# Head normalisation of two mixers: token-major outputs and accumulated squares in place of one-column TensorE sums

## The reference, cut to what matters

```python
# first mixer: HGRN2, 4 heads
o = o * lax.rsqrt(jnp.mean(o * o, axis=-1, keepdims=True) + EPS) * head_gain
o = o.reshape(B, S, HG_WIDTH) * jax.nn.silu(g_out)
# second mixer: 4 heads of differential attention, and 4 heads of retention done in the same way
o = jnp.einsum('bhqk,bkhd->bqhd', attn, v)
o = rmsnorm(o, subln_w) * (1.0 - lam_init)
```

## Time and profile before

| | |
|---|---|
| median of 3 runs | 2704.78 us |
| profiled execution | 2705.11 us |
| its span, first to last instruction | 2703.3 us |
| TensorE busy | 2682.1 us |
| VectorE busy | 1837.1 us |
| ScalarE busy | 1323.3 us |
| chain that ended last | 94% TensorE |
| granted TensorE clock, mean | 0.998, and 9 tenths or more in each of the page's 40 slices |

### The profile page before, as it was taken

How to read it: one execution, slowest core, us unless ns; L and a number is a source line. 1 busy time by engine, 2 the same in 40 slices (tenths; PEclk the granted TensorE clock), 3 DMA queues, 4 the chain that set the end, 5 groups by cost and what they waited for, 6 DMA issues and landing times.

```text
span 2703.3 us, 44352 instructions
## 1 busy us (share of the span) xinstructions
PE 2682.1 (99%) x17492; PEld 1727.2 (64%) x17492; DVE 1837.1 (68%) x2793; ACT 1323.3 (49%) x2116; POOL 139.1 (5%) x119
## 2 busy tenths in 40 slices
PE   9999999999999999999999999999999999999998
PEld 6886476654688646885476654688646555465554
DVE  7995385666899528993485665899436775557754
ACT  5664365552566425663365542566334644336352
POOL 1000021100100001000021100100000002000020
PEclk9999999999999999999999999999999999999999
DMA  5443322212344333443322223444233131321312
GB/s 168 109 123 105 121 63 71 90 63 102 94 119 114 121 104 96 109 115 110 120 68 63 83 78 102 125 110 123 105 121 110 63 94 63 125 67 63 110 63 86
DMA packets 317434, 266.18 MB, mean 98 GB/s; under 512 B 8908, under 2 KB 280524, under 8 KB 316656
## 3 DMA queue, kind: packets, MB, share of 16 engines
q1 hardware_dynamic: 314416, 254.57, 30.5%
q10 hardware_dynamic: 2272, 7.58, 1.1%
q0 software_dynamic: 608, 2.11, 0.3%
HBM read 257.40 MB, written 4.21 MB: 97 GB/s over the span
## 4 chain that ended last, share of the span: by engine, by line
PE 94%; DVE 3%; ACT 1%; DVEq 0%; issue 0%; DMA 0%; POOL 0%; ACTq 0%; SPq 0%
PE pu L463 14%; PE pu L464 14%; PE pu L465 14%; PE pm L465 6%; PE pm L463 6%; PE pm L464 6%; PE pu L595 6%; PE pu L594 6%; PE pu L596 6%; PE pm L594 2%; PE pm L595 2%; PE pm L596 2%; PE pm L905 2%; PE pm L666 2%; PE pm L892 1%; PE pm L697 1%
## 5 line engine op out<-in xcount | busy, mean ns | idle before, releaser
L1106 DVE SCALAR_TENSOR_TENSOR w_lo<-stage,w_hi 128x2048 f16<-128x2048 f32 (+1 forms) x156 | 353.2, 2264 | 358.1 <-ACT w_hi L1865 354.1
L1865 ACT ACTIVATE w_hi<-stage 128x2048 f16<-128x2048 f32 (+1 forms) x147 | 273.7, 1862 | 530.0 <-PE pm L465 378.2
L463 PE MATMUL pu<-h_hi,w_hi 128*128 128x512 f16 x912 | 346.3, 380 | 2.7 <-DVE w_lo L1106 2.7
L465 PE MATMUL pu<-h_hi,w_lo 128*128 128x512 f16 x912 | 345.6, 379 | 0.0
L464 PE MATMUL pu<-h_lo,w_hi 128*128 128x512 f16 x912 | 345.6, 379 | 0.0
L463 PE MATMUL pu<-w_hi,arena 128*128 128x512 f16 x512 | 194.0, 379 | 0.0
L464 PE MATMUL pu<-w_lo,arena 128*128 128x512 f16 x512 | 194.0, 379 | 0.0
L465 PE MATMUL pu<-w_hi,arena 128*128 128x512 f16 x512 | 194.0, 379 | 0.0
L463 PE MATMUL pm<-w_hi,arena 128*128 128x512 f16 x512 | 194.0, 379 | 0.0
L464 PE MATMUL pm<-w_lo,arena 128*128 128x512 f16 x512 | 194.0, 379 | 0.0
L465 PE MATMUL pm<-w_hi,arena 128*128 128x512 f16 x512 | 194.0, 379 | 0.0
(11 more groups left out here) (332 smaller groups left out, 6209.5 us busy)
## 6 DMA issues: line engine op xcount, KB each, us to landing
stage<-in_w_in_dram SPq DMA_DIRECT2D x136, 512.0 KB, 4.6
stage<-in_w_ffn_gate_dram SPq DMA_DIRECT2D x88, 512.0 KB, 4.0
stage<-in_w_ffn_up_dram SPq DMA_DIRECT2D x88, 512.0 KB, 5.2
stage<-in_w_ffn_down_dram SPq DMA_DIRECT2D x80, 512.0 KB, 4.0
stage<-in_w_out_dram SPq DMA_DIRECT2D x40, 512.0 KB, 4.2
stage<-in_w_in_dram SPq DMA_DIRECT2D x24, 256.0 KB, 3.2
stage<-in_w_ffn_down_dram SPq DMA_DIRECT2D x16, 256.0 KB, 4.1
stage<-in_w_branch_hgrn_dram SPq DMA_DIRECT2D x8, 512.0 KB, 3.6
```

Source lines behind the costliest of these rows:

```text
L463: nc.tensor.matmul(ps, w1, r_hi, start=first, stop=False)
L465: return nc.tensor.matmul(ps, w2, r_hi, start=False, stop=last)
L1106: V.scalar_tensor_tensor(out=w_lo[:, s, 0:n], in0=stage[:, s, 0:n], scalar=WSCALE, in1=w_hi[:, s, 0:n], op0=ALU.mult, op1=ALU.subtract).th ...
L1865: A.activation(w_hi[:, s, 0:n], stage[:, s, 0:n], ACT.Copy, scale=WSCALE).then_inc(hi_split, 1)
```

## The change

Both operands of the head's output product are exchanged: the scores are stationary, the values move, and the output has tokens in partitions. The 128 channels of a block then lie along the free dimension. ScalarE copies the output first and then squares it in 4 operations of 128 columns, each with an accumulated sum (`head_squares`), between two drains; `token_sums` is gone with its semaphore. The root now reads those sums. VectorE multiplies the copy by the reciprocal (`scale_head`), and TensorE turns the scaled output back with 4 transposes (`head_turn`), in the place of the 4 that spread the scale. VectorE's last step has one multiplication less.

```diff
@@ TensorE, first mixer
-                    last = nc.tensor.matmul(pm[2][:, b * P:], hV[:, b, hd * P:(hd + 1) * P], S[:, b, 0:T - b * P],
-                                            start=b == 0, stop=b == NB - 1)
+                    for kb in range(b + 1):
+                        last = nc.tensor.matmul(pm[2][:, b * P:(b + 1) * P], S[:, kb, (b - kb) * P:(b - kb + 1) * P],
+                                                hV[:, kb, hd * P:(hd + 1) * P], start=kb == 0, stop=kb == b)
-            def head_norm():
-                pe.wait_ge(o_sq, t.next("o_sq"))
-                token_sums(pm[3], sq[:, 0]).then_inc(o_ss, 1)
-
-            def head_scale(ps):
+            def head_turn(ps, src):
 
                 pe.wait_ge(o_rc, t.next("o_rc"))
-                over_partitions(ps, r_col[:, NB:]).then_inc(o_rb, 1)
+                for b in range(NB):
+                    last = nc.tensor.transpose(ps[:, b * P:(b + 1) * P], src[:, b * P:(b + 1) * P], ident[:])
+                last.then_inc(o_rb, 1)
@@ TensorE, second mixer
-                    last = nc.tensor.matmul(ps[:], v_tok[:, b, hd * P:(hd + 1) * P], AT[:, b], start=b == 0, stop=b == NB - 1)
+                    for kb in range(NB):
+                        last = nc.tensor.matmul(ps[:, b * P:(b + 1) * P], AT[:, kb, b * P:(b + 1) * P], v_tok[:, kb, hd * P:(hd + 1) * P],
+                                                start=kb == 0, stop=kb == NB - 1)
-                    if m == 1 and i % 4 == 3 and i > 3:
-                        pe.wait_ge(o_rt, t.next("o_rt"))
...
                 if q in (6, 10, 14, 18):
-                    head_norm2(pm[3])
+                    pe.wait_ge(o_sq, t.next("o_sq"))
@@ VectorE
-            def invert_head():
+            def scale_head(tile):
+
                 v.wait_ge(o_rt, t.next("o_rt"))
-                V.reciprocal(r_col[:, NB:], r_col[:, NB:]).then_inc(o_rc, 1)
+                V.reciprocal(r_col[:, NB:], r_col[:, NB:])
+                v.drain()
+                blocks = tile.rearrange("p (b d) -> p b d", b=NB)
+                V.tensor_tensor(blocks, blocks, r_col[:, NB:].unsqueeze(2).to_broadcast([P, NB, P]), ALU.mult).then_inc(o_rc, 1)
...
-                V.scalar_tensor_tensor(out=tc[:, 0], in0=sq[:, 1], scalar=lp[:, C_HG:C_HG + 1], in1=pm[3][:], op0=ALU.mult, op1=ALU.mult)
-                v.drain()
-                V.tensor_tensor(tc[:, 0], tc[:, 0], hgs[:, hd], ALU.mult)
+                V.scalar_tensor_tensor(out=tc[:, 0], in0=pm[3][:], scalar=lp[:, C_HG:C_HG + 1], in1=hgs[:, hd], op0=ALU.mult, op1=ALU.mult)
...
-                V.scalar_tensor_tensor(out=r_post[:], in0=tc[:, k % 2], scalar=gain, in1=r_post[:], op0=ALU.mult, op1=ALU.mult)
-                v.drain()
-                V.tensor_tensor(r_post[:], r_post[:], gate, ALU.mult)
+                V.scalar_tensor_tensor(out=r_post[:], in0=r_post[:], scalar=gain, in1=gate, op0=ALU.mult, op1=ALU.mult)
@@ ScalarE
+            def head_squares(tile):
+
+                s_.drain()
+                for b in range(NB):
+                    A.activation(sq[:, 0, b * P:(b + 1) * P], tile[:, b * P:(b + 1) * P], ACT.Square, accum_out=r_col[:, NB + b:NB + b + 1])
+                s_.drain()
+
             def mixer_slot(q):
...
-                    A.activation(sq[:, 0], pm[2][:], ACT.Square)
-                    A.activation(sq[:, 1], pm[2][:], ACT.Copy).then_inc(o_sq, 1)
+                    A.activation(sq[:, 1], pm[2][:], ACT.Copy)
...
+                if step == 0 and 1 <= hd <= HG_HEADS:
+                    head_squares(sq[:, 1])
                 if step == 1 and 1 <= hd <= HG_HEADS:
-                    s_.wait_ge(o_ss, t.next("o_ss"))
-                    root(r_col[:, NB:], pm[3][:, 0:NB], 1.0 / P).then_inc(o_rt, 1)
+                    root(r_col[:, NB:], r_col[:, NB:], 1.0 / P).then_inc(o_rt, 1)
```

More of the change, by code:

```diff
@@ L110 @@
             bias_ready=3, gp_land=48,
[L111 to L112 removed]
+            lev_pre=32, lev_exp=32, lev_done=32, off_done=4, o_done=4, o_rt=4, o_rc=4, o_rb=4, sc_done=8, mx_ready=8, ex_done=8, pt_done=8,
+            at_done=8, at_hi=8, s_clear=1, g_ready=2, lev_ready=32, lev_taken=32, off_taken=4, o_ready=4, at_ready=8, p_ready=8, pt_ready=8, m_ready=8)
 PER2 = dict(split=24, land0=32 * 12, land1=32 * 12, hi_split=24, unit_done=23, evac=MIX2_DVE, evac_a=MIX2_ACT, pre_act=2, act_done=2, y_park=4, y_done=4,
             dec_pre=4, dec_done=4, sc_done=16, mx_ready=16, ex_done=16, p_ready=16, pt_done=16,
[L115 removed]
+            pt_ready=16, o_rc=8, o_done=8, o_sq=8, o_rt=8, o_rb=8, o_cp=8, m_ready=12, rot_ready=2, rot_land=64, dup_land=32, ret_done=16, ret_ready=16, pw_land=16,
             pool_sum=1, pool_in=4, pool_done=4, pool_free=1, x_ready=4, rx=4, xn_ready=4, tp_done=8, hh_ready=8, h_ready=8)
@@ L473, in unit_ready @@
                     pe.wait_ge(evac, t.next("evac"))
[L475 to L485, removed]
             def in_step(ps, s, at, k):
@@ L753, in mixer_slot @@
                     head_out(hd - 1)
-                if step == 1 and 1 <= hd <= HG_HEADS:
-                    head_norm()
                 if step == 2 and 1 <= hd <= HG_HEADS:
-                    head_scale(pm[3])
+                    head_turn(pm[3], sq[:, 1])
                 if hd < HG_HEADS:
@@ L885, in scores2 @@
                     if m == 1 and i % 4 == 2 and i > 2:
-                        pe.wait_ge(o_sq, t.now("o_sq"))
+                        pe.wait_ge(o_sq, t.at("o_sq", i // 4))
                     if m == 1 and i in (8, 12):
                         pe.wait_ge(o_cp, t.next("o_cp"))
-                    if m == 1 and i % 4 == 3 and i > 3:
-                        pe.wait_ge(o_rt, t.next("o_rt"))
                     r = slice(64 * m, 64 * m + 64)
@@ L919, in retention_scores @@
                     r = slice(64 * ((hd + other) % 2), 64 * ((hd + other) % 2) + 64)
[L920 to L924, removed]
+                    if i == NB - 1 and hd == 0:
+                        pe.wait_ge(o_cp, t.next("o_cp"))
                     nc.tensor.matmul(pm[b][:], z[r, 2 + c, b * P:(b + 1) * P], z[r, c], start=True, stop=True).then_inc(ret_done, 1)
@@ L940, in mixer2_slot @@
                 if q in (7, 11, 15):
-                    head_scale(pm[1])
+                    head_turn(pm[1], tc[:, (q - 7) // 4 % 2])
                 if q == 19:
-                    head_scale(pm[3])
+                    head_turn(pm[3], tc[:, 1])
                 if q in (6, 10, 14, 18):
-                    head_norm2(pm[3])
+                    pe.wait_ge(o_sq, t.next("o_sq"))
                 hd, step = divmod(q - RET_SLOT, 2)
@@ L950, in mixer2_slot @@
                     if hd:
-                        head_norm2(pm[1])
+                        pe.wait_ge(o_sq, t.next("o_sq"))
                     else:
-                        pe.wait_ge(o_rt, t.next("o_rt"))
                         pe.wait_ge(rot_ready, t.next("rot_ready", 2))
@@ L962, in mixer2_slot @@
                     if hd:
-                        head_scale(pm[1])
+                        head_turn(pm[1], tc[:, (hd - 1) % 2])
                     head_out2(pm[0], bV, hd)
@@ L969, in mixer2_slot @@
                         if gr == 1:
-                            pe.wait_ge(o_rt, t.next("o_rt"))
-                            head_scale(pm[1])
+                            head_turn(pm[1], tc[:, 1])
                             pe.wait_ge(o_cp, t.next("o_cp"))
@@ L1455, in mixer_slot @@
                 if step == 1 and 1 <= hd <= HG_HEADS:
-                    invert_head()
+                    scale_head(sq[:, 1])
                 if step == 2 and 1 <= hd <= HG_HEADS:
@@ L1689, in mixer2_slot @@
                 if 0 < hd <= B_HEADS and step == 0:
-                    invert_head()
+                    scale_head(tc[:, (hd - 1) % 2])
                 between()
@@ L1719, in mixer2_slot @@
                 if q in (6, 10, 14, 18):
-                    invert_head()
+                    scale_head(tc[:, (q - 6) // 4 % 2])
                 if q == POOL_SLOT - 5:
@@ L2207, in mixer2_slot @@
                     s_.drain().then_inc(ex_done, 1)
-                if q in (5, 9, 13, 17) or (0 <= ret < B_HEADS and step == 1):
-                    ps, k = (pm[1], (q - 5) // 4) if q < RET_SLOT else (pm[0], A_HEADS + ret)
+                ends = q in (5, 9, 13, 17) or (0 <= ret < B_HEADS and step == 1)
+                ps, k = (pm[1], (q - 5) // 4) if q < RET_SLOT else (pm[0], A_HEADS + ret)
+                if ends:
                     if k >= 2:
@@ L2216, in mixer2_slot @@
                     taken(q - 1)
+                if ends:
+                    head_squares(tc[:, k % 2])
                 if q in (7, 11, 15):
@@ L2219, in mixer2_slot @@
                 if q in (6, 10, 14, 18) or (0 < ret <= B_HEADS and step == 0):
-                    s_.wait_ge(o_ss, t.next("o_ss"))
-                    root(r_col[:, NB:], pm[3 if q < RET_SLOT else 1][:, 0:NB], 1.0 / P).then_inc(o_rt, 1)
```

(1 more changed line is left out.)

5 lines of the change are left out of this document (removed).

## The result

The changed kernel takes 2712.18 us (median of 11 runs, 2710.33 to 2713.94), against 2704.78: a ratio of 1.0027, interval 1.0019 to 1.0035. The forecast of 2703.7 and its range (2691 to 2710) miss this on the slow side. The profiled execution took 2713.74 us, 1.6 more than the median, with a span of 2711.9, 8.6 more than the span before.

What follows compares the result with a forecast made beforehand. TensorE was taken as the bound, busy 2682.1 of 2703.3 us. Terms of -19.4, +2.0, +6.9, +1.0, +1.8 and +6.6 gave -1.1 us, from 2704.78 to 2703.7; range 2691 to 2710, likeliest "no difference".

Steps and rivals of the forecast that it cites:

- the sums: TensorE's one-column sums, 24 groups of 8 records, go: 0.81 us each, 19.4 us saved.
- shorter products: Heads' output products in both mixers, in more pieces of 128 columns: 0.1 and 0.05 us a head, 2.0 us more.
- wait at slot 17: HGRN2, slots 15 to 17: the turn waits for the later root and scaling, 3.45 us, twice, 6.9 us.
- wait at slot 12: HGRN2, slots 11 and 12: the turn waits for the scaled head, 0.5 us, twice, 1.0 us.
- wait at slot 19: TensorE waits for the copy of the turned result ahead of the last score product: 0.9 us, twice, 1.8 us.
- waits for `w_lo`: Slots 21 and 25, both layers: root and scaling delay the weights' low half, 1.65 us four times, 6.6 us.
- copies at slots 8, 12: Second score products waiting for ScalarE's copy of the turned head; the prediction had no term for it.
- clock: TensorE's granted clock behind the waits; the forecast sum had no term for a fall.
- the clock falls in the long wait of slot 17: Rival: some 3.8 us idle at slot 17 halves TensorE's clock, 4 us lost each time, +8 us, 2711.7; chance 0.05.
- The squares: ScalarE's four accumulated squares of a head with two drains: 1.86 us, moving the root that much later at slot 17.
- The cited rule on short products: Skill's 81 ns for 128 columns against 131 for 512: some 80 us lost; the prediction held the trace disagreed for float32.

Runs made afterwards that it cites:

- nosums_free: Kernel before without the one-column sums on TensorE (norm not computed) and without TensorE's waits for ScalarE's root: 2686.30 us, ratio 0.9927.
- swaponly: Kernel before with only the operands of the heads' output products exchanged in both mixers, sums kept: 2707.63 us, ratio 1.0007.
- fill17: Changed kernel with 28 float16 products of no use ahead of TensorE's wait at slot 17, both layers: 2708.89 us, ratio 1.0017 to the kernel before.
- nosums: Kernel before without the one-column sums on TensorE; the root reads its own last values, so the norm isn't computed: 2697.59 us, ratio 0.9972.
- lofirst: Changed kernel with VectorE's low-half split and retention multiplications ahead of its head scaling in slots 21, 23, 25, 27: 2700.88 us, ratio 0.9985 to the kernel before.
- rootnow: Changed kernel with ScalarE's root of the HGRN2 heads directly behind their squares, in step 0: 2710.75 us, ratio 1.0021 to the kernel before.
- turn18: Changed kernel with the third HGRN2 head turned and finished one slot later, in slot 18: 2700.99 us, ratio 0.9985 to the kernel before.
- combo: Changed kernel with turn18, lofirst and ScalarE's copy of a turned head ahead of the transposed probabilities in slots 7, 11, 15: 2694.30 us, ratio 0.9950 to the kernel before.
- rootnow2: rootnow, with VectorE also scaling the head ahead of its low-half weight split: 2702.02 us, ratio 0.9992 to the kernel before.
- combo2: combo, with VectorE also scaling the last attention head ahead of the rotation's final addition in slot 18: 2695.05 us, ratio 0.9959 to the kernel before.

## Why the prediction was wrong, step by step

Its sum against the profiled execution, term by term:

| term | predicted | found | from |
|---|---|---|---|
| the sums | -19.4 | -21.6 | 24 x 0.90, `nosums_free` |
| shorter products | +2.0 | +2.8 | 3.74 and 2.39 us; `swaponly` +2.6 |
| wait at slot 17 | +6.9 | +6.2 | 2 x (3.41 - 0.32) |
| wait at slot 12 | +1.0 | +0.7 | 2 x 0.36 |
| wait at slot 19 | +1.8 | +2.2 | 2.7 at the turn, less 0.5 for the copy before |
| waits for `w_lo` | +6.6 | +5.9 | 8.6 - 2.7: 7.1 in the second mixer, less 1.2 in the first |
| copies at slots 8, 12 | none | +2.5 | 4 x 0.63 |
| clock | none | +9.5 | 2.9 + 3.3 at slot 17, 3.3 at slot 19, each against `fill17` |
| sum | -1.1 | +8.2 | span: +8.6 |

- **The step that failed is the clock.** The waits were forecast well in sum: 17.5 us found, 16.3 forecast. But the kernel was taken to run at full clock behind them, a term put at nothing that measured 9.5 us. The rival "the clock falls in the long wait of slot 17" had this right in place and sign, with 8 us for the two where 6.2 were lost. That its 2711.7 is within 0.5 us of the median is in part luck: it has two falls of 4 us where three of about 3.2 came, and the misses of the other terms partly cancel.
- **The rival got its chance of 0.05 on a misreading.** The argument against it was that the 2.1 us wait of the earlier trace rows had left the clock at 9 tenths or more in each of the page's slices. A slice of that page is 2703.3/40 = 67.6 us long, and a fall of some microseconds doesn't show in it: the page of the changed kernel has a 9 in all 40 slices too, with three falls in them. The kernel before, at that very wait:

```profile
15.60 1.90 PE L500 MATMUL pu<-ident,arena 128*128 128x128 f32 x8 [2.14 <-DVE h_lo L1154]
```

```profile
15.00:20.00 5.00, 4.28 (x22) 3.28 (x23) 3.79 (x9) 4.23 (x9) 0.00 (x0) 0.66 0.95 283
20.00:25.00 5.00, 5.00 (x48) 4.48 (x47) 3.13 (x5) 1.11 (x3) 1.56 (x1) 1.00 0.43 125
```

The wait ends at 15.60 us, inside the stretch of 8 to 20 us that the prediction itself quoted at 0.72: the row that was to speak against the rival stood beside a fall. TensorE has other idle time in this opening, so the rows don't show that this one wait caused it; they do show that it was no evidence of a clock that holds. The rule that the prediction cited beside this rival (the Trainium skill, TensorE: Matmul & The Clock Gate, HAM oscillation — how this bites in real kernels), that pauses between bursts bring the slow clock back, agrees with the trace at slot 17: 1.00 before the wait, then the rows at 0.69 and 0.63. It doesn't explain the fall of `swaponly`, which came without a pause.

- **The sums were priced 0.09 us too low.** Where the difference lies isn't shown: in the earlier trace rows a group starts at 2125.39, and the next line's first product stands at 2126.20, 0.81 us later, as the prediction had it.
- **The squares were priced too high**, 1.86 us against 1.4, from another activation function: an accumulated Square comes every 0.3 us, an accumulated Exp every 0.39. At slot 17 the forecast moved the root 1.86 us later and TensorE 0.81 us earlier. Found: the root stayed, because ScalarE's list had come forward with TensorE by about what the squares cost, and TensorE came 2.3 us earlier. The wait was as long as forecast all the same. That is a hit with a wrong mechanism.
- **Slot 19 has the right size at another place.** The forecast put the wait ahead of the last score product, for the copy; it stands ahead of the turn, for VectorE's scaling. For `w_lo` 1.5 to 1.7 us were forecast four times; found were 2.60, 1.54, 1.45 and 1.53.
- **The copies at slots 8 and 12 were missed.** The prediction followed the turned head to VectorE, and not ScalarE's copy of it, which stands behind the transposed probabilities and gates the next score product.
- **The cited rule on short products** (the Trainium skill, TensorE: Matmul & The Clock Gate, Back-to-back issue gap; some 80 us by its ratio) did not come true for float32: 0.112 us a record of 128 columns, 2.8 us in all, as line 666 had let one expect.

## What to carry to other kernels

- Where a change takes work from the bound engine and lets it arrive earlier at the same gates, add up two things: the waits, and for the longer ones a chance of a fall of the clock, here mostly 2.9 to 3.3 us each. Look for falls in stretches of 5 us: a slice of the page hides them. Filling such a wait with products of no use gave the clock's part back at that place, though part of it was lost again further on; moving the late operation up in its engine's list gave both.
- When something that another engine reads becomes that engine's own (here sums by ScalarE, root by ScalarE), look where the old hand-over had put it in the lists. Here two such orders stood, the root and scaling of a head behind other work at slot 17, and a weight split behind the scaling in the retention slots; mending either gained 10 to 11 us, falls of the clock included, more than the whole change cost.
- Read the waits of weight loads beside those of products: 8.5 us of waits in `nosums` stood only there.

## What the runs showed of the hardware

- How often the clock fell, each from one profiled execution. Behind the waits of 3.4 us of slot 17: in both layers of the changed kernel and of `lofirst`, 4 of 4. Behind that of 2.9 us: in one layer of `rootnow`, 1 of 2. Behind 2.6 us for `w_lo`: in both layers of `fill17`, and once each not in the changed kernel, `turn18` and `rootnow`, 2 of 5. Behind the 1.36 us wait of slot 19: in layer 1 of the changed kernel and of `rootnow`, in layer 0 of `turn18`, in both layers of `combo` and `rootnow2`, and in neither of `lofirst` and `fill17`, 7 of 14. Behind waits of 1.4 to 1.6 us for `w_lo` in the changed kernel, `fill17`, `turn18`, `rootnow` and `rootnow2`: 0 of 15. So the length of the wait alone doesn't decide it, and in `swaponly` it fell with no wait at all.
- By the stretches between head outputs a fall costs 1.7 us (each of the two in `fill17`) to 3.3, in `turn18` 5.0.
- Executions of one kernel differ by several microseconds: `combo` 2689.2 or 2694 to 2696, `combo2` 2691.3 to 2691.4 or 2695.1. The kernel before does so too, 2703.4 to 2710.0 in 30 executions on one chip, so this spread is no sign of the new waits.
- Float32 loads of 0.19 us with every record of 128 columns are hidden down to 0.112 us a record.
